# A two-block transformer kernel: the odd layer's opening, with its first weight issued earlier and its token tiles handled ahead of its context tiles

## What is computed

```python
# end of layer 0: each row takes its two experts' weighted outputs
x = x + g2 * f[:B * S].reshape(B, S, D)
ctx = ctx + cg2 * f[B * S:].reshape(B, Lc, D)
# begin of layer 1
h = modulate(rmsnorm(x, norm_mix_g[l]), sh1, sc1)        # tokens
hc = modulate(rmsnorm(ctx, norm_mix_g[l]), csh1, csc1)   # context
q, k, v = jnp.split(h @ w_in, 3, axis=-1)
kc, vc = jnp.split(hc @ w_in[:, C_WIDTH:], 2, axis=-1)   # no query for the context
```

## Time and profile before

| | |
|---|---|
| time of the kernel, median of 3 runs | 2152.22 us (2151.64 to 2152.79) |
| the profiled execution: its span, first to last instruction | 2144.4 us |
| what lies around the span, against the median | 7.8 us |
| PE busy, DVE busy, ACT busy, POOL busy | 92%, 31%, 17%, 15% of the span |
| TensorE clock granted, mean | 0.984 |
| read from HBM over the span | 569.21 MB |

### The profile page before, as it was taken

How to read it: one execution, slowest core, us unless ns; L and a number is a source line. 1 busy time by engine, 2 the same in 40 slices (tenths; PEclk the granted TensorE clock), 3 DMA queues, 4 the chain that set the end, 5 groups by cost and what they waited for, 6 DMA issues and landing times.

```text
span 2144.4 us, 34236 instructions
## 1 busy us (share of the span) xinstructions
PE 1973.9 (92%) x14861; PEld 1233.5 (58%) x14861; DVE 658.1 (31%) x1532; ACT 371.1 (17%) x821; POOL 321.9 (15%) x264
## 2 busy tenths in 40 slices
PE   5999999999999869999999988988879989989998
PEld 4565565555555445546565444444457667675874
DVE  1334373222222231214441111111136031037742
ACT  3143410000000020123320000000021130042231
POOL 0124411000000000014410000000120060040120
PEclk9999999999999989999999999999989999999999
DMA  9352399999999976226299999999964423427221
GB/s 366 134 210 88 124 377 409 428 426 425 428 424 426 426 271 201 91 79 247 96 386 425 427 423 426 427 422 425 414 227 147 156 79 124 151 79 197 80 90 59
DMA packets 129906, 581.16 MB, mean 271 GB/s; under 512 B 19210, under 2 KB 30634, under 8 KB 105040
## 3 DMA queue, kind: packets, MB, share of 16 engines
q1 hardware_dynamic: 107184, 546.11, 63.9%
q10 hardware_dynamic: 16448, 26.33, 3.5%
q0 software_dynamic: 6112, 6.39, 0.9%
HBM read 569.21 MB, written 21.38 MB: 275 GB/s over the span
## 4 chain that ended last, share of the span: by engine, by line
PE 67%; DMA 22%; DVE 3%; issue 3%; POOL 2%; ACT 2%; SPq 1%; ACTq 0%; POOLq 0%; DVEq 0%
DMA RG<-in_moe_w 19%; PE banks L1544 13%; PE banks L2542 8%; PE banks L1569 6%; PE banks L2099 4%; PE banks L2544 4%; PE banks L1092 4%; PE banks L1520 3%; PE banks L683 3%; PE banks L2101 3%; PE banks L2743 3%; PE banks L2954 2%; POOL AR L920 2%; PE banks L813 2%; PE banks L341 1%
## 5 line engine op out<-in xcount | busy, mean ns | idle before, releaser
L1544 PE MATMUL banks<-RG,HT 128*64 128x256 f32 x3616 | 428.4, 390 | 34.7 <-DMA RG<-in_moe_w 32.6
L1544 PEld LDWEIGHTS banks<-RG,HT 128*64 128x64 f32 x3616 | 251.9, 135 | 217.9 <-DMA RG<-in_moe_w 54.7
L1774 POOL DMA_INDIRECT y_rows<-AR x64 | 63.8, 997 | 874.2 <-DVE AR L1583 873.3
L1553 DVE TENSOR_TENSOR AR<-AR,banks 128x256 f32<-128x256 f32 x64 | 38.6, 603 | 482.9 <-ACT AR L1549 431.7
L1569 PE MATMUL banks<-RG,AR 128*64 128x512 f32 x752 | 171.7, 598 | 4.5 <-DVE AR L1562 3.1
L2542 PE MATMUL banks<-HT,RG 128*128 128x256 f32 x768 | 168.0, 380 | 0.8 <-ACT HT L552 0.8
L2542 PEld LDWEIGHTS banks<-HT,RG 128*128 128x128 f32 x768 | 145.4, 190 | 22.8 <-issue 2.4
L1549 ACT ACTIVATE AR<-banks 128x256 f32<-128x256 f32 x64 | 24.6, 384 | 751.2 <-PE banks L1544 751.2
L1520 PE MATMUL banks<-AR 128*128 128x256 bf16 (+1 forms) x1152 | 147.7, 275 | 2.0 <-DVE AR L1508 1.5
L1520 PEld LDWEIGHTS banks<-AR 128*128 128x128 bf16 x1152 | 107.4, 98 | 33.0 <-issue 18.3
L1569 PEld LDWEIGHTS banks<-RG,AR 128*64 128x64 f32 x752 | 50.2, 136 | 94.9 <-issue 83.2
(11 more groups left out here) (483 smaller groups left out, 2433.4 us busy)
## 6 DMA issues: line engine op xcount, KB each, us to landing
RG<-in_moe_w SPq DMA_DIRECT2D x160, 2048.0 KB, 24.3
AR<-in_moe_w SPq DMA_DIRECT2D x32, 2048.0 KB, 13.2
RG<-in_ada_w SPq DMA_DIRECT2D x24, 2048.0 KB, 8.9
RG<-in_attn_w_in SPq DMA_DIRECT2D x20, 2048.0 KB, 7.6
RG<-in_odd_w_in SPq DMA_DIRECT2D x6, 2048.0 KB, 21.4
RG<-in_ssm_w_in SPq DMA_DIRECT2D x4, 2048.0 KB, 9.0
AR<-y_rows ACTq DMA_DIRECT2D x6, 1024.0 KB, 7.6
RG<-in_even_w_in SPq DMA_DIRECT2D x2, 2048.0 KB
```

Source lines behind the costliest of these rows:

```text
L1544: m = pe.matmul(p[64 * h:64 * h + 64, 256 * i:256 * i + 256], x[:, k, :], w[:, h, k], start=k == 0, stop=k == 7, skip_group_check=True)
```

## The change

PE no longer calls `experts_done`. SP's wait for the last row load and the eight bias loads move from before odd (0, 0) to before odd (1, 0). Tiles 0 and 1 are joined, normed, turned and evicted first. Tiles 2 and 3 are joined between the token tiles' evictions on DVE, and turned by PE after the second and third part of the query projection, into banks of their own (4 to 7). The query projection waits for tiles 0 and 1 only; the bias turns behind it wait for tiles 2 and 3. The keep matmuls become 36 in one run.

```diff
             pe_overflow(pe, E0)
-            experts_done(pe, E0)
...
         def odd_bank_of(t, k):
+            if t >= 2:
+                return PS[2 * t + k // 4], 128 * (k % 4)
             x = (0, 0, 0, 0, 1, 1, 2, 2)[k]
-            return PS[(4 + 2 * (t % 2), 5 + 2 * (t % 2), t % 2)[x]], 128 * (k - (0, 4, 6)[x])
+            return PS[(4 + 2 * t, 5 + 2 * t, t)[x]], 128 * (k - (0, 4, 6)[x])
...
         def pe_odd_begin(pe):
             pe_odd_cols(pe)
-            for t in range(4):
-                pe_keep(pe, (26, 4, 0, 0)[t], 3)
...
+            pe_keep(pe, 36, 3)
+            for t in range(2):
+                pe_odd_turn(pe, t)
...
         def act_odd_begin(act):
...
+            for i in range(2):
+                act_odd_squares(act, i)
+                act_root(act, ("mix1", i), at_=i)
+            act.wait_ge(*at("ada_cols", 1, 3))
+            for t in range(2):
+                act_odd_turned(act, t)
+            for i in range(2, 4):
+                act_odd_squares(act, i)
             act_root(act, ("mix1", 3), n=2, at_=2)
...
         def dve_odd_begin(v):
...
+            dve_odd_raw(v, 1)
+            dve_odd_cols(v)
+            for i in range(2):
+                dve_odd_join(v, i)
+            for i in range(2):
+                dve_rstd(v, ("mix1", i), D, at_=i)
+                dve_diagonal(v, i)
+            v.wait_ge(*at("ada_cols", 1, 3))
+            for i in range(2):
+                dve_odd_turned(v, i)
+                dve_odd_join(v, 2 + i)
             v.wait_ge(*at("squares", ("mix1", 2)))
             dve_rstd(v, ("mix1", 3), D, n=2, at_=2)
             for t in (2, 3):
                 dve_diagonal(v, t)
...
+            for t in (2, 3):
+                dve_odd_turned(v, t)
...
         def pe_odd(pe):
-            for b in range(2):
-                pe.wait_ge(*at(*turned_out("mix1", 3, b)))
+            for t in range(2):
+                for b in range(2):
+                    pe.wait_ge(*at(*turned_out("mix1", t, b)))
             for c in range(3):
                 for j in range(4):
                     pe_odd_part(pe, c, 0, j)
+                    if c == 0 and j in (1, 2):
+                        pe_odd_turn(pe, j + 1)
+                if c == 0:
+                    for t in (2, 3):
+                        for b in range(2):
+                            pe.wait_ge(*at(*turned_out("mix1", t, b)))
...
         def act_odd(act):
-            act.wait_ge(*at("turned", "mix1", 3, 1))
+            act.wait_ge(*at("joined_rows", 3))
...
                     act_odd_part(act, c, 0, j)
+                    if c == 0 and j in (1, 2):
+                        act_odd_turned(act, j + 1)
...
-                if key == ("odd", 0, 0):
+                if key == ("odd", 1, 0):
                     sp.wait_ge(*at("z_load3", 0))
                     sp_bias(sp)
```

More of the change, by code:

```diff
@@ L2006, in odd_bank_of, with pe_odd_turn @@
         def odd_bank_of(t, k):
+            if t >= 2:
+                return PS[2 * t + k // 4], 128 * (k % 4)
             x = (0, 0, 0, 0, 1, 1, 2, 2)[k]
-            return PS[(4 + 2 * (t % 2), 5 + 2 * (t % 2), t % 2)[x]], 128 * (k - (0, 4, 6)[x])
+            return PS[(4 + 2 * t, 5 + 2 * t, t)[x]], 128 * (k - (0, 4, 6)[x])
+        def pe_odd_turn(pe, t):
+            pe.wait_ge(*at("diagonal", t))
+            if t >= 2:
+                for b in range(2):
+                    pe.wait_ge(*at(*turned_out("mix1", t - 2, b)))
+            for k in range(8):
+                bank, c = odd_bank_of(t, k)
+                m = pe.matmul(bank[:, c:c + 128], XS[:, t, 128 * k:128 * k + 128], DG[t], start=True, stop=True,
+                              skip_group_check=True)
+                if k in (odd_on_act(t) - 1, 7):
+                    m.then_inc(*ev("turned", "mix1", t, k // 7))
@@ L2010, in pe_odd_begin @@
         def pe_odd_begin(pe):
             pe_odd_cols(pe)
-            for t in range(4):
-                pe_keep(pe, (26, 4, 0, 0)[t], 3)
-                pe.wait_ge(*at("diagonal", t))
-                for b in range(2):
[L2016 to L2023, removed]
+            pe_keep(pe, 36, 3)
@@ new lines, in pe_odd_begin, with act_odd_squares, act_odd_turned @@
+            for t in range(2):
+                pe_odd_turn(pe, t)
+        def act_odd_squares(act, i):
+            act.wait_ge(*at("joined_rows", i))
+            act.activation(E0.Z[i][:, 0, :], XS[:, i, :], ACT.Square,
+                           accum_out=ST[:, i:i + 1]).then_inc(*ev("squares", ("mix1", i)))
+        def act_odd_turned(act, t):
+            act.wait_ge(*at("turned", "mix1", t, 0))
+            for k in range(odd_on_act(t)):
+                bank, c = odd_bank_of(t, k)
+                ins = act.activation(HT[:, k, 128 * t:128 * t + 128], bank[:, c:c + 128],
+                                     ACT.Identity, scale=COLS[1][:, 1, t // 2, k:k + 1],
+                                     bias=COLS[1][:, 0, t // 2, k:k + 1])
+            ins.then_inc(*ev("turned_out", "mix1", t, 0))
@@ L2027, in act_odd_begin @@
             act.activation(ST[:, 62:63], IDN[:, 0:1], ACT.Sqrt)
[L2028 to L2033, removed]
-            act_root(act, ("mix1", 3), n=2, at_=2)
-            act.wait_ge(*at("ada_cols", 1, 3))
@@ L2045, in dve_diagonal, with dve_odd_turned @@
+            act.wait_ge(*at("ada_cols", 1, 3))
[3 more added lines that the diff above has]
+                act_odd_squares(act, i)
+            act_root(act, ("mix1", 3), n=2, at_=2)
         def dve_diagonal(v, t):
             v.tensor_scalar(DG[t], IDN[:], ST[:, 16 + t:17 + t], None, MUL).then_inc(*ev("diagonal", t))
-        def dve_odd_begin(v):
[L2049 to L2058, removed]
+        def dve_odd_turned(v, t):
+            v.wait_ge(*at("turned", "mix1", t, 1))
+            for k in range(odd_on_act(t), 8):
+                bank, c = odd_bank_of(t, k)
+                ins = v.tensor_scalar(HT[:, k, 128 * t:128 * t + 128], bank[:, c:c + 128],
+                                      COLS[1][:, 1, t // 2, k:k + 1], COLS[1][:, 0, t // 2, k:k + 1], MUL, ADD)
+            ins.then_inc(*ev("turned_dve", "mix1", t, 1))
@@ new lines, in dve_odd_join @@
+        def dve_odd_join(v, i):
+            v.wait_ge(*at(f"z_load{i}", 0))
+            dve_join(v, E0, i, ev("joined_rows", i))
+        def dve_odd_begin(v):
+            dve_odd_raw(v, 1)
[9 more added lines that the diff above has]
+                dve_odd_join(v, 2 + i)
```

## The result

The changed kernel took 2135.52 us (median of four runs, 2133.49 to 2137.47), against 2151.93 us for the kernel before in the same comparison (four runs, 2148.38 to 2152.79). The ratio is 0.9927, with a 95% interval of 0.9914 to 0.994.

A forecast was written before the change was run, and what follows sets the result against it. The prediction took the late first odd weight to bound the seam, some 6 us beyond the tokens. Terms: -13.0 earlier key projection, +2.5 contention, +1.0 clock = -9.5 us, so 2152.2 becomes 2142.7 us; range 2138.5 to 2147.5.

The forecast's parts named there:

- its sum: Layer 0 to odd layer seam: -13.0 + 2.5 + 1.0 = -9.5 us at the key projection.
- Contention: At the last scatter of expert rows: the early weight shares the DMA engines and delays the scatter, +2.5 us.
- the bound of 6.1: Upper limit for the scatter's delay: a gather's 9.4 us under full load against the scatter's 3.34, +6.1 us.
- The clock: PE's idle of some 2.6 us ahead of the first token turn may halve its clock: +1.0 us, between 0 and 2.05.
- PE's freed wait: PE without experts_done is free from 767.7; costed at nothing, since the first join waits for its row load until 781.29.
- I carry the 9.5 to the end: From the key projection to the kernel's end: PE releases every later stage, so the full 9.5 us gain stays.
- The starting point: The whole kernel's median, 2152.2 us, taken as 7.8 us above the profiled span of 2144.4.
- Contention free: Rival at the seam: the scatter takes its turn at once and the clock stays up; -13.0, 2139.2 us, chance 0.23.
- the scatter waiting out the weight: Rival at the seam: the scatter is delayed by all of 6.1 us, turn in half clock; -4.8, 2147.4 us, chance 0.20.
- Absorbed later: Rival in layer 1: its expert weight stream starts no earlier and eats the whole gain; 2152.2 us, chance 0.05.
- The slower rival: Rival in the query projection: PE stays at 1.2 GHz through its parts and turns, +17.9 us; 2160.6 us, chance 0.04.

The follow-up runs named there:

- the two second profiles: Both kernels profiled again without an edit: the changed kernel 2136.56 us (five runs), the kernel before 2148.81 us (one run).
- before's second profile: The kernel before, unchanged, profiled a second time: one run, 2148.81 us, span 2147.0.
- the new order alone: The changed kernel with the first odd weight issued behind SP's last-row-load wait and bias loads again: 2150.95 us, ratio 1.0002 to the kernel before.
- the second comparison: The changed kernel timed again without an edit: 2136.56 us (five runs) against 2149.71 for the kernel before (27 runs), ratio 0.9947.
- the wait put back: The changed kernel with PE's wait for the expert rows restored ahead of its ada products: 2136.96 us, ratio 0.9944 to the kernel before.

## Why the prediction was wrong

**The seam: its sum was right.** The forecast for this profiled run was a query projection at 791.8 + 2.5 + 1.0 = 795.3 and a key projection at 818.8, that is 27.6 and 51.1 us behind the last down projection (767.7). The two profiles of the changed kernel have 28.1 and 27.8, and 51.3 and 50.9. As a gain it is 9.3 us against the profile that the forecast was made from and 11.0 between the two second profiles. What was to be seen was seen: no wait of PE for the weight, the scatter between 4.5 and 7.5 us (5.99 and 6.2), SP's first odd issue near 757 (759.80, right behind the ada issues, which end 3.1 us later in this execution than in the earlier trace rows). No turn stalled PE inside the projection.

**Two terms were off and cancelled, which is luck.** Contention was put at +2.5. Against the first profile of before the second row load landed 4.0 us later (13.6 to 17.6 behind the last down projection), of which 1.5 is that profile's short scatter; against before's second profile it is 1.8 to 2.5, of which the scatter is 1.2 to 1.4 and the rest isn't shown to be contention. The Trainium skill, page "DMA: Bandwidth & Descriptors", section "Queues, rings and completion order", says that an engine alternates between its queues packet by packet. The measured 0.7 to 1.4 us on the scatter is nearer to that than to the bound of 6.1, which was read from a gather. The clock was put at +1.0 and cost nothing in the two turns: the gap ahead of them was 0.21 us, since the conditioning products ran later than I had them (up to 781.4 instead of 776, because PE stopped twice on the way, 3.61 and 1.27 us, and did them at half clock, in 7.4 us where the new order alone took 4.0 at 2.4 GHz). The upper bound of that term was too small: I had counted one tile's turn, 2.05 us, and in the profile with six keep calls fewer the half clock cost 2.9 in the turns and 1.7 in the projection.

**PE's freed wait: costed at nothing, measured at nothing** (2136.96 against 2136.56), to within the 3 us of the intervals. PE's own stops took up most of what the freed wait gave (the products end 1.3 us earlier, not 3.7), and the first row load, which the first join waits for, lands behind them in both profiles of the changed kernel.

**The step that failed is "I carry the 9.5 to the end".** Half of the miss of 7 us is here. The stages between the key projection and the second block did keep the gain, but the last stage did not keep its length. Its start is taken from the keep matmuls that open the second block (1578.15 in before, 1569.90 in the changed kernel); from there to the end of the span it is 566.2 and 565.2 us in the two profiles of before, 561.8 and 562.4 in those of the changed kernel: -3.6 us. That is the stop of 1.75 us and the half clock of 1.7 behind it, and it goes with the number of instructions, not with the seam's order: six keep calls alone remove it from the kernel before (-3.4 us), and six fewer bring the stop back in the changed kernel's profile. I had counted the added keep calls as 1.4 us of PE's waiting time and as nothing else; all instructions behind them were moved as well.

**The starting point was off, too.** I set the sum against the median 2152.2 and took 7.8 us as lying around the span. With the distance of 1.8 us that every listed run has, the run that was profiled took 2144.4 + 1.8 = 2146.2; it was 6 us faster than the median, and the sum of terms read from it needn't hold against the others. With seam and end, each as the mean of the two profiles of either kernel, the working gives -10.1 - 3.6 = -13.7 us; the second comparison, with 27 runs of before, has 2149.71 - 2136.56 = 13.2. The first has 16.4. The 3.2 between them are the two medians' own movement (2.2 in before's, 1.0 in the changed kernel's), which I don't attribute further.

**The rivals.** Contention free and the scatter waiting out the weight are both off: the scatter is longer by about 1 us, not 0 and not 6. Absorbed later is off: the middle of the kernel, from the key projection to the second block's opening, takes 748.6 to 752.9 us in all the profiles, without a trend. The slower rival's mechanism exists in a small form: the first two query parts ran at half clock for a while in several of these kernels, at a cost of 1.7 to 2.8 us and not of 17.9.

## What to carry to other kernels

Move a stage's first weight ahead of the waits of the stage before as soon as its slot is free, and put what that weight needs first in front of the rest: the order pays only once the weight is there. A change of a few instructions moves every instruction that follows on its engine: look for short stops without a releaser elsewhere in the profile, and time one kernel that is only padded, before a gain or a loss is ascribed to the edit. And read the profiled run's own time beside its span, and a second profile of before, since one of them may hold a short transfer or be quicker than the median.

## What was not expected of the hardware

- PE can stop in the midst of equal instructions while it waits for nothing that the profile shows. In the stop of the kernel before, the DMA queue that carries instructions moved one packet (view of the queues, 2073.5 to 2076.5: queue, kind, packets, MB, share of 16 engines):

```profile
q8 instruction: 1, 0.02, 2.1%
```

  while the queue of the weight loads filled 90.6% there. In the changed kernel such a packet lies in 2061 to 2064.8, ahead of the 64 products:

```profile
q8 instruction: 1, 0.02, 3.5%
```

  The Trainium skill, page "Runtime: NRT & Kernel Launch", section "Instruction fetch mechanics", says that an engine's instructions come in blocks of 16 KiB and that crossing a block is mostly hidden. The packet's 0.02 MB agrees with the size; if the stop is such a crossing, it was not hidden here, at 1.75 us and 1.7 us of half clock behind it. That PE stops for its own instructions, with a fetch that comes late, is argued from the packet; that the stop goes by the instruction count is shown by the two kernels with six keep calls more and fewer. Why 24 instructions are enough to hide it, and whether the weight loads delay it, was not tried.
- The same scatter of rows took 3.34 us in the first profile of before and 4.83 to 4.88 in the five others where no odd weight was put beside it, and 5.50 to 6.2 beside an early weight.
- After 2.0 to 2.7 us of idle PE sometimes kept 2.4 GHz (the changed kernel, 2.46 us of idle: two parts in 7.15 us, granted clock 1.00 from 797 to 799) and sometimes fell to half of it (the wait put back, 2.47 us: 8.83, granted clock 0.50 from 798 to 800).
